# The q, k, v and memory projections run as fourteen jobs inside the recurrent branch

## The reference

```python
h = rms_norm(x, attn_norm[l])
proj = h @ w_in[l]
q_da, k_da, v_da, rw_cols, q_mem = jnp.split(proj, [c1, c2, c3, c4], axis=-1)
...
o_da = diff_attention(q_da, k_da, v_da, positions, da_q_norm[l], da_k_norm[l], lam, lam_init, da_subln[l])
o_rw = rwkv7_time_mix(rw_cols, rw_mu[l], rw_w0[l], rw_w2[l], rw_a0[l], rw_a2[l], rw_g2[l],
                      rw_k_k[l], rw_k_a[l], rw_r_k[l], rw_gn_w[l], rw_gn_b[l])
mem_n = rms_norm(mem, mem_norm[l])
o_mem = memory_attention(q_mem, mem_n, w_mem_kv[l], mem_q_norm[l], mem_k_norm[l])
mixed = jnp.concatenate([o_da, o_rw.astype(o_da.dtype), o_mem], axis=-1)
x = x + mixed @ w_out[l]
```

```python
sa = jnp.einsum('bhvk,bhk->bhv', state, -kk_t)
state = (state * w_t[:, :, None, :]
         + sa[..., None] * (kk_t * a_t)[:, :, None, :]
         + v_t[..., None] * k_t[:, :, None, :])
y = jnp.einsum('bhvk,bhk->bhv', state, r_t)
```

## Time and profile before

| | |
|---|---|
| median of 3 runs | 1765.39 us (1764.23 to 1765.56) |
| the profiled execution | 1765.87 us, span 1764.1 us |
| TensorE busy | 1600.3 us, 91% |
| VectorE, ScalarE busy | 1025.1 us, 811.5 us |
| mean granted TensorE clock | 0.926 of full speed |
| weight loads of 512 KB | 549, median 5.0 us from issue to landing |

### The profile page before, as it was taken

How to read it: one execution, slowest core, us unless ns; L and a number is a source line. 1 busy time by engine, 2 the same in 40 slices (tenths; PEclk the granted TensorE clock), 3 DMA queues, 4 the chain that set the end, 5 groups by cost and what they waited for, 6 DMA issues and landing times.

```text
span 1764.1 us, 29387 instructions
## 1 busy us (share of the span) xinstructions
PE 1600.3 (91%) x10556; PEld 1458.6 (83%) x10556; DVE 1025.1 (58%) x1544; ACT 811.5 (46%) x1323; POOL 41.7 (2%) x50
## 2 busy tenths in 40 slices
PE   6477858699999999999998799999999999999997
PEld 6376857488988886999897689999899988889997
DVE  3543466478878884555543745555555554555554
ACT  4311535277767773334443444433434444553342
POOL 1030000000000000000000100000000000000000
PEclk9586969899999999999998589999999999699999
DMA  6941422179979994555453055555455544055552
GB/s 241 158 51 52 152 72 72 36 279 346 349 254 352 346 352 155 192 192 186 143 179 108 1 179 176 181 178 180 155 191 188 178 143 144 15 168 192 189 188 72
DMA packets 83687, 308.04 MB, mean 175 GB/s; under 512 B 9246, under 2 KB 9374, under 8 KB 83360
## 3 DMA queue, kind: packets, MB, share of 16 engines
q1 hardware_dynamic: 79632, 289.97, 47.6%
q0 software_dynamic: 3552, 15.84, 4.8%
q10 hardware_dynamic: 432, 1.26, 0.2%
HBM read 299.69 MB, written 7.34 MB: 174 GB/s over the span
## 4 chain that ended last, share of the span: by engine, by line
PE 84%; DVE 8%; ACT 4%; issue 2%; DMA 1%; POOL 0%; DVEq 0%; SPq 0%; ACTq 0%; POOLq 0%
PE ps L1381 24%; PE ps L1382 23%; PE ps L1383 23%; PE ps L1387 3%; PE ps L1489 2%; DVE w_lo L848 1%; PE ps L1461 1%; PE ps L1549 1%; ACT arena L554 1%; PE ps L1624 1%; DMA raw<-in_wstream 1%; ACT w_hi L519 1%; DVE xT_lo L876 1%; PE ps L1701 1%; ACT arena L560 1%
## 5 line engine op out<-in xcount | busy, mean ns | idle before, releaser
L848 DVE TENSOR_TENSOR w_lo<-raw,w_hi 128x1024 fp32r<-128x1024 f32 x549 | 646.2, 1221 | 301.6 <-ACT w_hi L519 300.4
L519 ACT ACTIVATE w_hi<-raw 128x1024 fp32r<-128x1024 f32 x549 | 549.4, 1056 | 228.8 <-PE ps L1383 190.2
L1381 PE MATMUL ps<-xT_hi,w_hi 128*128 128x256 f32 x1656 | 470.2, 284 | 4.7 <-DVE xT_lo L876 4.0
L1382 PE MATMUL ps<-xT_lo,w_hi 128*128 128x256 f32 x1656 | 468.6, 283 | 0.0
L1383 PE MATMUL ps<-xT_hi,w_lo 128*128 128x256 f32 x1656 | 468.6, 283 | 0.0
L1381 PEld LDWEIGHTS ps<-xT_hi,w_hi 128*128 128x128 f32 x1656 | 317.6, 192 | 10.6 <-issue 7.1
L1382 PEld LDWEIGHTS ps<-xT_lo,w_hi 128*128 128x128 f32 x1656 | 317.6, 192 | 3.1
L1383 PEld LDWEIGHTS ps<-xT_hi,w_lo 128*128 128x128 f32 x1656 | 317.6, 192 | 0.0
L1381 PE MATMUL ps<-w_hi,xT_hi 128*128 128x256 f32 (+2 forms) x848 | 261.4, 308 | 13.0 <-issue 8.4
L1382 PE MATMUL ps<-w_lo,xT_hi 128*128 128x256 f32 (+2 forms) x848 | 251.9, 297 | 0.0
L1383 PE MATMUL ps<-w_hi,xT_lo 128*128 128x256 f32 (+2 forms) x848 | 251.7, 297 | 0.0
(11 more groups left out here) (292 smaller groups left out, 1357.0 us busy)
## 6 DMA issues: line engine op xcount, KB each, us to landing
raw<-in_wstream SPq DMA_DIRECT2D x549, 512.0 KB, 5.0
bias_tiles<-arena POOLq DMA_DIRECT2D x2, 3072.0 KB, 52.6
arena<-bias_tiles POOLq DMA_DIRECT2D x2, 3072.0 KB, 14.0
const<-in_const ACTq DMA_DIRECT2D x1, 1112.0 KB, 10.3
smallw<-in_smallw POOLq DMA_DIRECT2D x1, 1104.0 KB, 5.4
x_res<-in_x SPq DMA_DIRECT2D x2, 512.0 KB, 4.4
arena<-in_mem POOLq DMA_DIRECT2D x1, 1024.0 KB, 5.4
out<-arena SPq DMA_DIRECT2D x2, 512.0 KB, 2.7
```

What stands on the lines that cost most here:

```text
L519: nc.scalar.activation(w_hi[:, slot, lo:hi], raw[:, slot, lo:hi], ACT.Copy).then_inc(S_(f"hi_{part_}"), 1)
L848: tt(w_lo[:, slot, lo:hi], raw[:, slot, lo:hi], w_hi[:, slot, lo:hi].bitcast(F32), ALU.subtract).then_inc(S_(f"lo_{part_}"), 1)
L1381: a = mm(out_, stat_[0], mov[0], start=start, stop=False)
L1382: b = mm(out_, stat_[0], mov[1], start=False, stop=False)
```

## The change

The 14 tiles of slots 3 to 7 and the 4 of slots 8 and 9 no longer go through `proj`. A slot becomes two jobs, one for each 128 tokens (`side_proj(n, t)`), in banks 6 and 7 alone: ten jobs for slots 3 to 7 and four for slots 8 and 9. They stand between the recurrent branch's steps: slot 3 before the gram blocks, (4,0) before gram block 1, (4,1) and (5,0) before the inversion, (5,1) and (6,0) in the state's first half, (6,1) and slot 7 after its second half. ScalarE and VectorE split the slots at places of their own.

The recurrent tiles arrive in the order 6, 7, 2, 3, 0, 1, 4, 5 and are shifted in pairs or singly as they come. The tables `prow` and `smallw` are reordered on the host, so that `final_g` and `wq` come last: their room holds v, the memory query and the memory's keys and values until the attention is over, and they are loaded behind it. q is kept in `mixed`. The memory is loaded and its squares are taken during the branch. The constants are loaded by GpSimd behind slot 0. The two bias stores go behind the first attention scores. The head norms of q and k are separated from those of the memory.

```diff
@@ the tables @@
+RW_TILES = (6, 7, 2, 3, 0, 1, 4, 5)
...
-for _name, _n in (("gn_w", 256), ("gn_b", 256), ("final_g", 1024), ("b_router", 20), ("sinks", 16)):
+for _name, _n in (("gn_w", 256), ("gn_b", 256), ("b_router", 20), ("sinks", 16), ("final_g", 1024)):
...
-for _name, _n in (("w2a2", 256), ("g2", 256), ("wq", 1536), ("router", 160)):
+for _name, _n in (("w2a2", 256), ("g2", 256), ("router", 160), ("wq", 1536)):
@@ GpSimd @@
-            pool.wait_ge(S_("raw_d1"), 32)
-            pool.dma_start(smallw[:, :], smallw_in).then_inc(S_("smallw_loaded"), 16)
-            pool.dma_start(prow[:, :], prow_in.partition_broadcast(P)).then_inc(S_("prow_loaded"), 16)
+            pool.wait_ge(S_("raw_d0"), 16)
+            pool.dma_start(const[:, P:CONSTW], const_in[:, P:CONSTW]).then_inc(S_("const_loaded"), 16)
+            at_wq, at_gain = SMALLW["wq"][0], PROW["final_g"][0]
+            pool.dma_start(smallw[:, 0:at_wq], smallw_in[:, 0:at_wq]).then_inc(S_("smallw_loaded"), 16)
+            pool.dma_start(prow[:, 0:at_gain], prow_in[0:at_gain].partition_broadcast(P)).then_inc(S_("prow_loaded"), 16)
...
-            pool.wait_ge(S_("vec_ready"), 1)
-            for v in range(2):
-
-                row = vec_sb[0:16, v, P - 1:P]
-                pool.dma_start(bias_dram[v], bass.AP(row.tensor, row.offset, [list(row.ap[0]), [-1, P], [1, 3 * P]])
-                               ).then_inc(S_("vec_stored"), 16)
...
-            pool.wait_ge(S_("rw_y"), 1)
+            pool.wait_ge(S_("inv_mm"), 2 * (len(LEVELS) - 1))
             pool.dma_start(mem_sb[:, :, :], mem_in.rearrange("(t p) d -> p t d", p=P)).then_inc(S_("mem_loaded"), 16)
-            for i in (1, 2, 3):
+            inverse_rms(1)
+            pool.wait_ge(S_("att_scores"), 1)
+            for v in range(2):
+
+                row = vec_sb[0:16, v, P - 1:P]
+                pool.dma_start(bias_dram[v], bass.AP(row.tensor, row.offset, [list(row.ap[0]), [-1, P], [1, 3 * P]])
+                               ).then_inc(S_("vec_stored"), 16)
+            pool.wait_ge(S_("att_out"), ATT1[1] // QUAD)
+            pool.dma_start(smallw[:, at_wq:SMALLWS], smallw_in[:, at_wq:SMALLWS]).then_inc(S_("smallw_loaded"), 16)
+            pool.dma_start(prow[:, at_gain:PROWS], prow_in[at_gain:PROWS].partition_broadcast(P)).then_inc(
+                S_("prow_loaded"), 16)
@@ ScalarE @@
+            def side_out(n, t):
+
+                act.wait_ge(*((S_("d_used"), n + 1) if t else (S_("side_psum"), n - QKV0 + 1)))
+                tiles = side[n]
+                for view in {id(v): v for v, _ in tiles}.values():
+                    cols = [c for v, c in tiles if v is view]
+                    j = [v is view for v, _ in tiles].index(True)
+                    w = P * len(cols)
+                    ins = nc.scalar.activation(view[:, t, cols[0]:cols[0] + w], ps[:, 6 + t, P * j:P * j + w], ACT.Copy)
+                ins.then_inc(S_("side_out"), 1)
...
+                if i < len(PIECES):
+                    split_hi(QKV0 + 3, "abd"[i])
+            side_out(QKV0 + 2, 1)
+            split_all(QKV0 + 4)
+            side_out(QKV0 + 3, 0)
+            norm_squares(1, ("mem_loaded", 16))
             act.wait_ge(S_("rw_var"), 1)
...
+            side_out(QKV0 + 3, 1)
+            split_all(MEM0)
+            for t in range(T):
+                side_out(QKV0 + 4, t)
+            norm_hi(1)
+            split_all(MEM0 + 1)
+            for t in range(T):
+                side_out(MEM0, t)
+            split_all(OUT0)
@@ VectorE @@
+            def shift(*tiles):
+
+                for i, k in enumerate(tiles):
+                    tt(rw_d[:, i, 1:S], rw_x[:, k, 0:S - 1], rw_x[:, k, 1:S], ALU.subtract)
+                    ins = ts(rw_d[:, i, 0:1], rw_x[:, k, 0:1], -1.0, None, ALU.mult)
+                link(ins)
+                for i, k in enumerate(tiles):
+                    ins = stt(rw_x[:, k, :], rw_d[:, i, :], pc("mu")[:, k:k + 1], rw_x[:, k, :], ALU.mult, ALU.add)
+                return ins
@@ TensorE @@
+            def side_proj(n, t, c=None):
+
+                job, s = side_job(n, t), n % 2
+                if job >= T:
+                    pe.wait_ge(S_("side_out"), job - 1)
+                else:
+                    pe.wait_ge(S_("evacuated"), evac_until(RW0 + 1))
+                wv = [w[:, s, :].rearrange("p (k c) -> p k c", k=KD) for w in (w_hi, w_lo)]
+                w = P * len(side[n])
+                for k in range(KD):
+                    if not t and k in PIECE_STEPS:
+                        for half in ("hi", "lo"):
+                            pe.wait_ge(S_(f"{half}_{PIECE_STEPS[k]}"), n + 1)
+                    transposed(c, k)
+                    last = mm3(ps[:, 6 + t, 0:w], [x[:, k, P * t:P * t + P] for x in (xT_hi, xT_lo)],
+                               [v[:, k, 0:w] for v in wv], k == 0, k == KD - 1)
+                    if t and k in (2, 5):
+                        last[2].then_inc(S_("a_used" if k == 2 else "b_used"), 1)
+                last[2].then_inc(S_("d_used" if t else "side_psum"), 1)
...
+            proj(RW0 + 2)
             pe.wait_ge(S_("rw_kksq"), 1)
...
+            side_proj(QKV0, 0)
+            side_proj(QKV0, 1)
             pe.wait_ge(S_("elem_done"), 1)
...
                 if c:
+                    side_proj(QKV0 + 1, 0)
                     pe.wait_ge(S_("gram_masked"), c)
...
+            side_proj(QKV0 + 1, 1)
+            side_proj(QKV0 + 2, 0)
             pe.wait_ge(S_("gram_masked"), T)
...
                 ins.then_inc(S_("rw_rhs"), 1)
+                if c == 0:
+                    side_proj(QKV0 + 2, 1)
...
                 ins.then_inc(S_("rw_out"), 1)
+                if c == 0:
+                    side_proj(QKV0 + 3, 0)
+            side_proj(QKV0 + 3, 1)
+            for t in range(T):
+                side_proj(QKV0 + 4, t)
+            norm(1, ("side_out", T * N_QKV))
+            pe.wait_ge(S_("xt_lo"), 4 + 3)
+            for n in range(MEM0, OUT0):
+                for t in range(T):
+                    side_proj(n, t, 1 if n == MEM0 and not t else None)
```

More of the change, by code:

```diff
@@ L304, in psum_places @@
         def psum_places(n):
-            pair = 4 + 2 * ((n - max(b for b in (RW0, QKV0, MEM0, OUT0, HYB0, HOUT0, SWA0, SOUT0) if b <= n)) % 2)
+            pair = 4 + 2 * ((n - max(b for b in (RW0, OUT0, HYB0, HOUT0, SWA0, SOUT0) if b <= n)) % 2)
             tiles = projections[n]
@@ L321, in psum_places, with side_job @@
             return pair, n_first, places
+        homes = ([(q_da, 128 * j) for j in range(4)] + [(k_da, 128 * j) for j in range(4)]
+                 + [(v_da, 128 * j) for j in range(4)] + [(qm, 128 * j) for j in range(2)])
+        side = {QKV0 + i: homes[3 * i:3 * i + 3] for i in range(N_QKV)}
+        homes = [(mkv, 128 * j) for j in range(4)]
+        side.update({MEM0 + i: homes[3 * i:3 * i + 3] for i in range(N_MEM)})
+        def side_job(n, t):
+            return T * (n - QKV0) + t
         units = []
@@ L522, in proj @@
             def proj(n, evacuate=True):
[L523 removed]
+                if n + 1 < N_SLOTS and n >= OUT0:
                     for part_ in PIECES:
@@ L541, in proj, with split_all, norm_squares @@
                 last.then_inc(S_("evacuated"), 1)
+            def split_all(n):
+                for part_ in PIECES:
+                    split_hi(n, part_)
+            def side_out(n, t):
[7 more added lines that the diff above has]
+                ins.then_inc(S_("side_out"), 1)
             def norm(c, wait=None):
+                norm_squares(c, wait)
+                norm_hi(c)
+            def norm_squares(c, wait=None):
                 n = norms[c]
@@ L558, in norm, with norm_hi @@
                         split_hi(0, "a")
+            def norm_hi(c):
+                n = norms[c]
+                if n["norm"]:
                     act.wait_ge(S_("rstd_ready"), normed[c] + 1)
-                    nc.scalar.activation(scaled[:, 1, :], n["src"][:, 1, :], ACT.Copy, scale=rstd[:, 1:2]).then_inc(
-                        S_("xs1_ready"), 1)
+                    nc.scalar.activation((mem_sb if c == 1 else scaled)[:, 1, :], n["src"][:, 1, :], ACT.Copy,
+                                         scale=rstd[:, 1:2]).then_inc(S_("xs1_ready"), 1)
                     if c == 0:
@@ L1090, in _ @@
             tt(two["sq"], two["kk0"], two["kk0"], ALU.mult).then_inc(S_("rw_kksq"), 1)
-            for part_ in PIECES:
-                split_lo(QKV0, part_)
+            link(shift(0, 1))
+            split_all(QKV0)
+            dve.wait_ge(S_("lam_exp"), 1)
+            link(tt(nlam, lame[:, 1:2], lame[:, 0:1], ALU.subtract))
+            link(ts(nlam, nlam, -LAM_INIT, None, ALU.add))
             dve.wait_ge(S_("rw_sig"), 1)
@@ L1207, in _ @@
             link(tt(ys, ys, y2, ALU.add))
-            dve.wait_ge(S_("vec_stored"), 32)
-            tt(mixed[:, :, 512:768], yt, g_tok, ALU.mult).then_inc(S_("rw_y"), 1)
-            for n in range(QKV0, MEM0):
-                proj(n)
```

(27 more changed lines are left out.)

213 lines of the change are left out of this document (113 added, 100 removed).

## The result

The changed kernel takes **1712.11 us** (median of 4 runs, 1711.62 to 1713.43) against 1765.47 beside it (1764.23 to 1767.95): a ratio of 0.9697, 95% interval 0.968 to 0.9714. The profiled execution's span fell from 1764.1 to 1710.0, by 54.1. Forecast were 1720.8 and a range of 1703 to 1734. On the three chips used for the experiments, repeated runs of the kernel before fell into two groups some 17 us apart (3 of 13, 14 of 17 and 4 of 22 runs under 1757; one more run of it, of 5295 us, and one of 6951 us of a variant are left aside), and the four runs of it shown here are all of the longer kind; runs of the changed kernel were of one kind only.

A forecast was written before the change was run, and what follows sets the result against it. The prediction took TensorE to bound the kernel nearly everywhere except its first 251 us. Gain 59.6 up to attention less about 15 for the stores' collision is 44.6, giving 1720.8 us, range 1703 to 1734.

The forecast's parts named there:

- Start: At the kernel's start, without the constants on ScalarE's queue, the first weight piece lands 2.8 us earlier (ends 1.5 and 3).
- Element stage: Recurrent branch before the gram blocks: tiles shifted pair by pair as they arrive, ending at 59.6 against 71.5, gain 11.9.
- Gram: Gram blocks and masks, with side jobs filling waits: inversion begins at 87.3 against 98.3, gain 11.0.
- State: The state's two halves after inversion, with jobs between: end at 146 (ends 144 and 151) against 160.0, gain 14.
- Projections and head norms: After the state: memory projections end at 179.9 against 231.9; attention starts at 191.7 against 251.30, gain 59.6.
- Rival 4: Recurrent branch: eight side jobs each exposed on the chain by 1.5 us more, 12 us, time 1733; chance 0.19.
- Collision: Output projection: bias stores delay slot 12's d part, holding TensorE 13.2 us; loss about 15, bounds 0 and 20.
- rival 2: Output projection: weights share with the bias stores from the first packet on, hold 7.3, time 1715; chance 0.16.
- Everything after slot 12 unchanged: Stages behind slot 12 gain or lose nothing, so the net gain stays 59.6 − 15 = 44.6 us.
- case 1: Whole kernel: time comes out as forecast, 1714 to 1728; chance 0.50.

The follow-up runs named there:

- slot 12 cured alone: The changed kernel with the sync queue's loop issuing slot n's d part ahead of slot n+1's a and b parts: 1767.88 us.
- the variant: The changed kernel with the second bias store issued behind the inverse norm of the expert stage: 1692.01 us, repeated on another chip 1689.84 us.

## Why the prediction was right, and where it was off

- **Start**: 2.6 measured, 2.8 forecast. Right.
- **Element stage**: last product over at 59.5, forecast 59.6. The walk through three in-order queues, with durations from rows, ended within 0.1 us, and VectorE's full 15.09 of 15.50 says that it was the right engine to walk.
- **Gram**: inversion from 85.8, forecast 87.3, and rounds of 6.1 from the first on. Right, 1.5 on the cautious side.
- **State**: last y copy at 148.7, forecast 146 with ends 144 and 151. The second half fell back to the low clock (0.68), which I had allowed for with 2 us and which took 5.
- **Projections and head norms**: memory projections ended at 180.7 (179.9 forecast), first score at 192.5 (191.7): 58.8 against 59.6, and 190.4 to 194.4 in five more traces of this code. Right. Rival 4, exposed jobs, would have put it at 204.
- **Collision**: the mechanism, its place and its signature were right: ScalarE waits for slot 12's d part between 244 and 266, TensorE with it. The size was off: 15 forecast, 22.4 in this trace against the kernel before, 17.5 to 22 by the experiments, and this trace passed the stated bound of 20. The step that failed is "Without the 2 MB of small tables that stood ahead of them (5 us at 0.4 MB per us) the stores end about 64 us after attention's start". They landed after 35.4 and 67.2 us, where it had been 37.0 and 68.2 in the earlier trace rows, so the tables ahead of them had cost them 1 to 2 us and not 5: the second landed 69 after attention's start, and TensorE restarted at 268.83, 76.3 after it, where 70.2 was forecast. It had stopped at 252.4, 59.8 after (57.0 forecast: the attention took 37.6 us at a clock of 0.64 where it had taken 33.9 at 0.83, and the projection behind it made up 0.9). So the hold is 16.5 and not 13.2, and 3.0 more (1.5 for slot 13's next part, and the low clock), where 1.6 was forecast, follow it: 2.9 + 16.5 + 3.0 = 22.4. The Trainium skill (DMA: Bandwidth & Descriptors, "Queues, rings and completion order") has each engine serve its queue rows in turn, a packet each. From 252 on the trace agrees (81 against 79 packets); for the 15 us before that it does not (9 packets of the sync queue from 237 to 252, against 314 of GpSimd's), and rival 2, which rested on the sharing alone, falls.
- **Everything after slot 12 unchanged**: the sentence that failed without harm. The code is unchanged, its time is not: 14.8 us in the last attention and 2.6 in the hybrid one come with a higher clock of TensorE. Without them the time would be about 1712.1 + 14.8 + 2.6 = 1729.5, 9 over the forecast, most of it the collision's 7.4; that is still in the range of 1703 to 1734, but no longer in case 1. So the nearness of 1712 to the forecast is partly luck, two errors of opposite sign. Against the four shorter runs of the kernel before beside it (1750.3 to 1752.7) the changed kernel's 1711.8 is a gain of 39 to 41, where 44.6 was forecast.

Whether the change frees the last attention from the low clock, or only shifts it to where chance is better, stays open. Of the changed kernel and its variants all nine profiles have 99.8 to 100.0 us there; of four profiles of the kernel before and its variants three have 114.6 to 117.6 and one 100.0. What was not tried: a delay in the middle of the program, and one of 40 us.

## What to carry to other kernels

A large store that nobody waits for is not free where it is put: ask which transfers fall due within its length, and put it into a stretch of idle DMA engines that is longer than it. One 3 MB store in each of two such stretches instead of both in one was worth 22 us here. Look at what stands behind the late part on every in-order engine, too: with slot 12 cured alone, slot 13's splits kept 12.6 of 22 us. And compare a stage of unchanged code in both traces before crediting its gain to the change: here 17 of 54 us came with the clock.

The best version measured is the changed kernel with the second bias store behind norm 3: 1689.84 us.

## What the runs showed of the hardware

- With 3 MB stores in flight on GpSimd's queue, the first issue on the sync queue took 0.33 us and the next ones 3.7 to 4.3, and the first packets moved some 13 us after the first issue. It showed in both kernels, at 53 us and at 237 us. Between the stores of the variant (235 to 253) nine issues took 0.33 us each and landed after 3.5 to 5.8 us.
- A store of 3 MB from 16 partitions takes 35 us alone, at some 97 GB/s, with the 16 DMA engines busy 0.95 of the time (195 to 225 and 260 to 290 in the variant's trace).
- In an attention stage TensorE's granted clock averaged 0.52 over 35 us in which TensorE was busy 35.00 us; it made 163 matmuls there, where 229 were made at 0.95. The 40 us after norm 9 agreed to the instruction in both cases.
- Which of the two happened went with the run and the chip, as far as times tell: 3 of 13, 14 of 17 and 4 of 22 runs of the kernel before were of the shorter kind.
